# The sparse attention layer in one block: a single stream of weight panels, attention units between its tiles, and the block compression in 32 products

## The reference, cut to what matters

```
kv = h @ w_kv                       # six parts of 256 columns: kc_raw, vc_raw, ks, vs, kw, vw
kc = silu(blocks(kc_raw) @ w1_k) @ w2_k   # blocks of 32 tokens at a stride of 16: 15 blocks x (32*64), + position rows
vc = silu(blocks(vc_raw) @ w1_v) @ w2_v
q, gates = h @ w_in                 # 16 heads of 64 in 4 groups; 3 gates per head
for each branch (compressed, selected, window):
    p = softmax(q k^T / 8 + bias[distance, head]) * mask
    o += sigmoid(gate) * p v
h = alpha * h + o @ w_o
```

## Time and profile before

| | us |
|---|---|
| median of 3 runs | 2943.93 (2943.51 to 2945.63) |
| the profiled execution | 2944.11 |
| its span in the profile | 2941.9 |
| share of the span in which PE is busy | 89% |
| DVE, ACT busy | 60%, 38% |
| the sparse attention layer, from 736.8 to 1098.7 us of the span | 361.9 |

### The profile page before, as it was taken

One profiled execution on the slowest core, in us unless ns is written; L12 is line 12 of the kernel. 1 busy time (PEld: TensorE's weight loads), 2 busy tenths in 40 slices (PEclk: granted clock), 3 DMA queues, 4 the chain that ended last, 5 costly groups with the idle time before them and its releaser, 6 DMA issues. The chain is left out here.

```text
span 2941.9 us, 46907 instructions
## 1 busy us (share of the span) xinstructions
PE 2611.1 (89%) x19241; PEld 2473.2 (84%) x19241; DVE 1750.7 (60%) x2584; ACT 1125.0 (38%) x1638; POOL 69.7 (2%) x120
## 2 busy tenths in 40 slices
PE   7838559998798775999799999999999999999998
PEld 7728549998796454999799988999999998899998
DVE  6455427776301433777577666657777765665776
ACT  4411234333402433433343355443343335554333
POOL 1000000000000000000000210000000021000000
PEclk9969869999855786999999999999999999999999
DMA  7400105553840011555255552345545555233552
GB/s 226 129 0 1 57 3 198 193 181 115 203 80 0 0 58 57 176 188 193 79 186 176 159 152 87 104 144 187 171 143 173 175 155 146 89 112 131 186 171 86
DMA packets 304981, 372.92 MB, mean 127 GB/s; under 512 B 15289, under 2 KB 275730, under 8 KB 304674
## 3 DMA queue, kind: packets, MB, share of 16 engines
q1 hardware_dynamic: 300848, 362.80, 38.7%
q0 software_dynamic: 3616, 7.89, 1.3%
q10 hardware_dynamic: 370, 0.11, 0.0%
HBM read 362.92 MB, written 7.86 MB: 126 GB/s over the span
## 5 line engine op out<-in xcount | busy, mean ns | idle before, releaser
L294 PE MATMUL psum_banks<-source_high,weights_high 128*128 128x272 f32 (+1 forms) x3744 | 1094.9, 292 | 99.9 <-DVE weights_low L478 52.8
L296 PE MATMUL psum_banks<-source_high,weights_low 128*128 128x272 f32 (+1 forms) x3744 | 1083.4, 289 | 0.0
L295 PE MATMUL psum_banks<-source_low,weights_high 128*128 128x272 f32 (+1 forms) x3744 | 1083.3, 289 | 0.0
L294 PEld LDWEIGHTS psum_banks<-source_high,weights_high 128*128 128x128 f32 x3744 | 722.9, 193 | 110.1 <-DVE weights_low L478 55.6
L295 PEld LDWEIGHTS psum_banks<-source_low,weights_high 128*128 128x128 f32 x3744 | 723.3, 193 | 0.2
L296 PEld LDWEIGHTS psum_banks<-source_high,weights_low 128*128 128x128 f32 x3744 | 722.5, 193 | 0.0
L294 PE MATMUL psum_banks<-hidden_high,weights_high 128*128 128x272 f32 (+1 forms) x1216 | 349.8, 288 | 0.0
L296 PE MATMUL psum_banks<-hidden_high,weights_low 128*128 128x272 f32 (+1 forms) x1216 | 348.5, 287 | 0.0
L295 PE MATMUL psum_banks<-hidden_low,weights_high 128*128 128x272 f32 (+1 forms) x1216 | 347.3, 286 | 0.0
L1004 DVE TENSOR_TENSOR weights_low<-weight_ring,weights_high 128x2048 fp32r<-128x2048 f32 x131 | 292.9, 2287 | 73.4 <-ACT weights_high L998 73.3
L998 ACT ACTIVATE weights_high<-weight_ring 128x2048 fp32r<-128x2048 f32 x131 | 242.5, 1912 | 195.9 <-PE psum_banks L296 184.5
(11 more groups left out here) (409 smaller groups left out, 3130.2 us busy)
## 6 DMA issues: line engine op xcount, KB each, us to landing
weight_ring<-ffn_w_in SPq DMA_DIRECT2D x88, 1024.0 KB, 6.4
weight_ring<-w_in SPq DMA_DIRECT2D x48, 1024.0 KB, 5.3
weight_ring<-ffn_w_out SPq DMA_DIRECT2D x44, 1024.0 KB, 4.9
weight_ring<-moe_w_gate SPq DMA_DIRECT2D x32, 1024.0 KB, 5.9
weight_ring<-moe_w_up SPq DMA_DIRECT2D x32, 1024.0 KB, 7.0
weight_ring<-moe_w_down SPq DMA_DIRECT2D x32, 1024.0 KB, 4.9
weight_ring<-gdn_w_in SPq DMA_DIRECT2D x16, 1024.0 KB, 6.3
weight_ring<-w_branch SPq DMA_DIRECT2D x12, 1024.0 KB, 5.0
```

Of the source, the lines that this page charges most:

```text
L294: pe.matmul(out, w_hi, x_hi, start=start, stop=False)
L295: pe.matmul(out, w_hi, x_lo, start=False, stop=False)
L296: return pe.matmul(out, w_lo, x_hi, start=False, stop=stop)
```

## The change

`HybridTiles` becomes `TileStream` with its sizes as arguments; for the mixer of the second block its instructions stay the same. `Unit` and `attention_phase` go, and `nsa_layer` is written anew as one block that also takes in the product with w_o. A stream of 14 panels feeds 28 tiles: w_kv (its parts in the order 0, 1, 2, 4, 3, 5), w_q and w_o. The small work stands between the tiles; of the eight tiles of w_q four come before the attention and four (18 to 21) in its first units. The compression contracts over two positions at once (128 rows) and holds four groups and the position row in 75 columns: 16 products for keys and 16 for values. The bias of the compressed keys is taken from the 128 x 256 picture, so `dist_up` and its 60 products go. The picture is made by GpSimd's DMA queue, started after tile 3. The compressed branch takes 8 heads per unit (4 units instead of 8). A group's three branches add up in one PSUM bank, both halves of the partitions, and are split straight from it into the source of w_o. The gate is a Tanh instead of a Sigmoid.

```diff
-    linear(i["nsa_w_kv"], 6 * NSA_G * NSA_D)
+    for part in NSA_KV:
+        linear(i["nsa_w_kv"], NSA_G * NSA_D, c0=part * NSA_G * NSA_D)
...
+NSA_KV = [0, 1, 2, 4, 3, 5]
+NSA_VT, NSA_Q, NSA_OUT, NSA_TILES = 12, 14, 22, 30
+NSA_FILL = {2: [18], 3: [19], 4: [20], 5: [21]}
...
+    for pair in range(2):
+        units += [SparseUnit(t, pair, None) for t in range(2)]
+        units += [SparseUnit(t, g, br) for g in (2 * pair, 2 * pair + 1) for t in range(2) for br in range(2)]
...
+            def _(sp):
+                for s, name in enumerate(("cmp_k_", "cmp_v_")):
+                    sp.dma_start(w1[:, s], i[name + "w1"].rearrange("(l q) c -> q l c", q=P)).then_inc(load.sem, 16)
...
+                load_ahead(pr, sp)
...
+            def _(pool):
...
+                pool.memset(hid_v[:, :, :], 0.0).then_inc(ready.sem, 1)
...
+                pool.wait_ge(act_n.sem, act_n.at(1))
+                pool.dma_start(pr.bias_dram.rearrange("p h x -> h p x"), bias_row[:, :].unsqueeze(1).to_broadcast([NSA_H, P, BIAS_W])).then_inc(pr.bias_out.sem, 16)
+                pool.wait_ge(pr.bias_out.sem, pr.bias_out.at(16))
+                pool.dma_start(bias[:, :, :], pr.view(pr.bias_dram, P - 1, [[NSA_H * BIAS_W - 1, P], [BIAS_W, NSA_H], [1, SEQ]])).then_inc(pr.bias_in.sem, 16)
...
+                def compress():
...
+                        for l in range(CMP_BLOCK // 2):
+                            mm = pe.matmul(ps[:, S_B, s * P:s * P + 75].rearrange("p (g n) -> p g n", n=NC), w1[:, s, l, :],
+                                           raw[:, s, :, 2 * l:2 * l + CMP_STRIDE * (NC - 1) + 1:CMP_STRIDE],
...
+                    else:
+                        for j in range(4):
+                            half, a = slice((j % 2) * NSA_D, (j % 2) * NSA_D + NSA_D), j // 2
+                            mm = pe.matmul(ps[:, S_B + j % 2, a * SEQ:a * SEQ + x.keys], q[half, 2 * x.group + a, at],
...
+                def weigh(u):
+                    x = units[u]
+                    if not x.last:
+                        return
+                    pe.wait_ge(ts.sem, ts.at(u + 1))
+                    if outs[u]:
+                        pe.wait_ge(ol.sem, ol.at(outs[u]))
+                    for r in range(2):
+                        o = ps[r * NSA_D:(r + 1) * NSA_D, O_B, 0:2 * P].rearrange("p (a q) -> p a q", a=2)
+                        for br in range(2):
+                            for b in range(x.t + 1):
+                                mm = pe.matmul(o, v_tok[:, br, b, x.group * NSA_D:(x.group + 1) * NSA_D], turned[:, br, b, r:4:2, :],
...
+                            for a in range(2 - 2 * br):
+                                pe.matmul(o[:, a, :], v_cmp[:, 4 * x.group + 2 * a + r, :], turned_cmp[:, 2 * (x.group // 2) + x.t, :],
...
+                for t in range(4):
+                    gemm(t)
+                tables()
+                for t in range(4, 8):
+                    gemm(t)
+                compress()
+                for t in range(8, 10):
+                    gemm(t)
+                compressed()
+                for t in range(10, 12):
+                    gemm(t)
+                gates()
...
+                for t in range(NSA_Q, NSA_Q + 4):
+                    gemm(t)
...
+                for u in range(n_units):
+                    if u + 2 < n_units:
+                        scores_of(u + 2)
+                    for t in NSA_FILL.get(u, []):
+                        gemm(t)
+                    if u:
+                        weigh(u - 1)
+                    turn(u)
+                weigh(n_units - 1)
+                pe.wait_ge(ol.sem, ol.at(outs[-1]))
+                for t in range(NSA_OUT, NSA_TILES):
+                    lin.multiply(pe, t, o_hi, o_lo)
...
+            def _(dve):
...
+                dve.wait_ge(pr.bias_in.sem, pr.bias_in.at(32))
+                max_of(0)
+                max_of(1)
+                normalise(0)
+                for u in range(n_units):
+                    if u + 2 < n_units:
+                        max_of(u + 2)
+                    for t in NSA_FILL.get(u, []):
+                        take(t)
+                    if u:
+                        out_low(u - 1)
+                    if u + 1 < n_units:
+                        normalise(u + 1)
...
         nsa_layer(pr)
-        residual_linear(pr, acc, SEQ, pr.x, pr.x, ALPHA)
         mix_norm(pr, 1)
```

More of the change, by code:

```diff
@@ L2125 @@
-N_UNITS = len(FILL)
-class HybridUnit:
-    def __init__(self, n):
-        self.branch, at = n // 6, n % 6
-        self.meta = at >= 4
-        self.qt, self.hg = (None, at - 4) if self.meta else (at // 2, at % 2)
-        self.parts = 1 if self.meta else 2
-        self.keys = META if self.meta and self.branch == 2 else L
-        self.by_act = self.branch == 0 or (self.meta and self.branch == 2)
-        self.dve_evicts = not self.by_act
-        self.act_evicts = self.by_act or not self.meta
@@ L2154, in __init__ @@
             self.ends.append(len(self.tiles))
-            if len(self.tiles) in (VT_CA, VT_B):
-                self.tiles += [None] * (2 if len(self.tiles) == VT_CA else 3)
+            self.tiles += [None] * gaps.get(len(self.tiles), 0)
             pr.used.append((pr.split_lo, pr.split_lo.at(p + 1)))
         self.n_panels = n_panels
-        by_dve = [b <= t < b + KT for t in range(N_TILES) for b in [max([x for x in BRANCH_TILES if x <= t], default=99)]]
-        self.by_dve = [d or t >= OUT_TILES for t, d in enumerate(by_dve)]
-        self.taken_by_dve = [sum(self.by_dve[:t + 1]) for t in range(N_TILES)]
+        self.stop = self.first + n_panels + (1 if hands_on else 0)
+        n = len(self.tiles)
+        self.by_dve = [by_dve(t) for t in range(n)]
+        self.taken_by_dve = [sum(self.by_dve[:t + 1]) for t in range(n)]
         self.taken_by_act = [t + 1 - n for t, n in enumerate(self.taken_by_dve)]
@@ L2170, in close @@
         pr.split_lo.passed(self.n_panels)
-        pr.tiles += N_TILES
+        pr.tiles += len(self.tiles)
         pr.taken_act.passed(self.taken_by_act[-1])
@@ L2177, in next_panel @@
         tile = self.tiles[t]
-        return tile[0] + 1 if tile and tile[1] == 0 else None
+        return tile[0] + 1 if tile and tile[1] == 0 and self.first + tile[0] + 1 < self.stop else None
     def high(self, act, p):
@@ new lines, with __init__ @@
+N_UNITS = len(FILL)
+class HybridUnit:
+    def __init__(self, n):
+        self.branch, at = n // 6, n % 6
+        self.meta = at >= 4
+        self.qt, self.hg = (None, at - 4) if self.meta else (at // 2, at % 2)
+        self.parts = 1 if self.meta else 2
+        self.keys = META if self.meta and self.branch == 2 else L
+        self.by_act = self.branch == 0 or (self.meta and self.branch == 2)
+        self.dve_evicts = not self.by_act
+        self.act_evicts = self.by_act or not self.meta
```

668 lines of the change are left out of this document (345 added, 323 removed).

## The result

The changed kernel takes 2776.01 us (median of 4 runs, 2774.93 to 2777.30) against 2944.78 us for the kernel before on the same chip (4 runs): ratio 0.9427, 95% interval 0.9411 to 0.9444. The profiled execution has a span of 2773.1 us, 168.8 less than before; 162.9 were forecast.

The account below looks back on a forecast made before the run. PE's order of work and the waits inside it were taken to bound the layer, DMA once. 71.9 + 7.4 + 95 + 24.7 = 199.0 us against 361.9, 162.9 less, gives 2781 us; range 2760 to 2822.

Parts of the forecast that it names:

- Up to the first scores: Layer start at 736.8 us to first scores: tiles, compression 7.7 us (bounds 6.7 to 15.4), gates, turns; 71.9 us, so 808.7.
- The fourth panel: Early tiles: small loads shrink to 2.5 MB, the panel lands at about 755 us, and ACT's 10.4 us stall goes.
- The picture: Bias picture written from 758.5 us and read back beside the panels, ready at 817 us, between 802 and 847.
- Now it shares them with the panels ... 45.5 us: Picture's write: 26.4 us of full engines at a 0.58 share take 45.5 us, plus 3 latency; alone it took 33.4.
- each is asked for some 18 us or more before it is needed, so no stall: Panels beside the picture's write: landing after 17.8 us as in an earlier row, they delay nothing.
- The 7.4 us wait of DVE: Before the first attention unit: DVE, ready at 809.6 us, waits for the picture until 817.
- That a panel could be late: Listed sign that the forecast is wrong: a panel is late while the picture is written; no size given.
- The attention: 4 pooled and 16 real units with four fill tiles: 95 us at an assumed clock of 0.8.
- the sum for 1.00: Attention at full clock: DVE 70 us, waits 12, filling and emptying 5, together 87 us.
- DVE is the fullest, but it cannot run through: Attention: DVE's 70 us are interrupted because its low part waits for values product and ACT's copy; 12 us over four groups.
- The end of the layer: Tiles 22 to 29: the 6.0 us of splitting source and panel go, the 24.7 us of tiles stay.
- Behind the layer: Everything after the layer: nothing outside it is touched, so no change in time was counted.

## Why the prediction was right, and where it was not

By its own sum the span of the profiled execution was put at 2779.0 us (2941.9 - 162.9) and was 2773.1, 5.9 less. Term by term:

- **Up to the first scores**: 808.7 forecast, 811.8 measured, 3.1 late. The compression is 8.5 us instead of 7.7 (0.133 us a record; "some more for the columns" was too little), within its bounds, at clock 1.00. PE waits 1.9 us ahead of the turns of the values. The fourth panel is not waited for, as forecast.
- **The picture**: the step that failed. "Now it shares them with the panels ... 45.5 us" made the picture pay for the sharing; the write landed after 33.4 us, no slower than alone. The panels paid: 27.7 us to landing, and "each is asked for some 18 us or more before it is needed, so no stall" was wrong by a 7.0 us wait of ACT. The 7.4 us wait of DVE did not come. That a panel could be late was named under what would make the forecast wrong; leaving the picture out puts its price at 4.5 us ahead of the scores, so this term was 7.4 for 4.5 with the mechanism turned round, and that the two sizes are close is luck. That price is inside the first point: without it the scores would have come 1.4 us ahead of the forecast.
- **The attention**: 95 forecast, 87.7 measured. The clock was 0.90, not 0.8; the sum for 1.00 had been 87. The 95 does not follow from its terms: added up as for 1.00 (DVE 70, waits 18, filling 5) they give 93. DVE is busy for 62.7 us instead of 70, the wait of its low part is 15.8 instead of 12. "DVE is the fullest, but it cannot run through" is what the runs show: 14.8 us more of DVE cost 6.7, 10.3 us more of busy PE cost 7.3 at the same clock, one buffer fewer costs 33.6 us, and the later low part gives 1.5 to 2 at the same clock. Not priced at all, though assumed by the model, was the third buffer.
- **The end of the layer**: no source and panel to split; PE is idle for 0.9 us before tile 22. From the last low part to the norm behind the layer it is 24.1 us, where 24.7 and the 1.0 up to that norm had been put: 1.5 less.
- **Behind the layer**: 7.2 us given back; the prediction said that nothing outside was touched. The instructions are the same. The stretch takes 1842.2 us before and with two buffers (2799.4 - 956.96 = 1842.4), and 1845.1 to 1849.7 in the other kernels with the change. The same 16 records of L527 take 3.72 or 5.41 us, so part of it is when the clock falls in a stage in which PE pauses often. It is not all: with rows of 1536 bytes they take 3.72 us and the stretch still 1846.9. The rest was not tried, and stays open.

The errors of the terms: +3.1, -7.4, -7.3, -1.5, +7.2, in all -5.9 us. They cancel in part, 10.3 us one way and 16.2 the other; that the sum is so near is partly luck.

On GpSimd's queue, the row shows 1.06 and 1.17 us for the two issues where SP had 0.35, and the write landed as soon as SP's. The Trainium skill, page "SBUF — State Buffer", section "SBUF: two separate sides", speaks against that queue because its descriptors wait for VectorE's two-port instructions. This case does not test the rule: VectorE ran nothing from 755.8 to 759.4 us nor from 782.4 to 796.4, so neither issue met one of its instructions, and the 0.7 and 0.8 us more per issue have another reason. What made the hardware queue better was the panels' share.

## What to carry to other kernels

A transfer that shares full DMA engines need not be the one that comes late: ask who else has an issue outstanding in that time and what waits for it, and price both. In a chain of units that goes round several engines, price the number of buffers before the busy times: one fewer cost 33.6 us, while 14.8 us of extra work on the fullest engine cost 6.7. Before a few us are put down to an edit, compare stretches at the same granted clock: the same attention took 86.0 and 86.1 us at 0.94, and 87.4 to 88.0 at 0.90. To learn what a stretch has to spare, double something in it: of 8.4 us of added products 4.5 vanished, and that was the wait's true size.

## What the runs showed of the hardware

- A write of 3.14 MB (3064 KB) to DRAM from 16 partitions in rows of 1532 bytes takes 32.9 to 33.6 us in either kind of queue, alone or beside panels, with rows of 1536 bytes too; an eighth of it takes 5.4 us. While it runs, the engines are full at 91 to 135 GB/s in all; in most slices after it about 350 (the GB/s line above). Why is open.
- Beside it, 1 MB panels land after 27.7 us when it is in GpSimd's queue (packets of 4.4 KB) and 22.7 in ScalarE's (1.5 KB), against 5.2 without it.
- The fill by full-array tiles was not needed for the clock: units without it kept 0.89 over the attention (0.90 with it).
